# Fourier and pooling products in pieces inside the attention stage of a mixer and mixture-of-experts model

## The chip, the cores and the metric

The kernel runs on one core of one Trainium2 chip. The metric is the device time of one execution in microseconds, lower is better. All arrays are 32-bit floats, and TensorE carries out each product of the program as two instructions.

## The reference

Two blocks follow each other, and the change lies in the first. That block has two layers. A layer works on 256 tokens `x` of width 1024 and on 256 context tokens `ctx` (the second layer updates `x` alone). Cut to the part around the change:

```python
px_all = hx @ w_in[i]                       # columns: 256 Fourier, 256 pool, 512 q, 256 k, 256 v
ax = blocked_attention(qx, k_all, v_all)    # 4 query heads of 128, 2 key and value heads, 512 keys
ox = jnp.concatenate([fourier_mix(px_all[..., F_OFF:P_OFF], w_fourier[i]),
                      pool_mix(px_all[..., P_OFF:Q_OFF], w_pool[i], pool_scale[i]),
                      ax], axis=-1) @ w_out[i]
x_new = x + g1 * ox
x_new = x_new + g2 * expert_choice_ffn(modulate(x_new, norm2_g[i], sh2, sc2), ...)

def fourier_mix(f, w):      # 4 heads of 64: real part of a 2-D DFT over (tokens, head width), then @ w
    fr = jnp.real(jnp.fft.fft2(fh, axes=(-2, -1), norm="ortho"))
    return fr @ w
def pool_mix(p, w, scale):  # 4 groups of 64: mean over a window of 2, 4, 8, 16 tokens minus p, then @ w
    ...
    return y * scale
```

In the first layer the context goes through the same operations with its own 256 keys. The second block (an RWKV and mLSTM mixer with two feed-forward parts, two layers) is not touched.

## The kernel before

The program is a list of stages. Each stage is one block: every engine has its own instruction stream in it, and a barrier over all engines closes it. `block1` (line 1230 on) calls for each layer `opening_stage`, `heads_project_stage`, `attention_stage` (line 591), `fourier_pool_stage` (line 724) once for each stream of tokens (two in the first layer, one in the second), `mix_route_stage` and `moe_stage`.

Weights come through a ring of seven places of 2 MB. The order of the tiles is fixed in `build_tiles`. SyncE issues the load of a tile (line 205) when TensorE has used the tile that held its place: it waits on the semaphore `used`, which only products count up. Loads of small arrays (`dft_n`, `pool_m`, `w_fourier`, `w_pool`) are issued by ScalarE in `heads_project_stage`, before attention.

`attention_stage` goes through jobs. A job is one head and 128 query tokens: in the first layer 8 jobs over 512 keys (`kt` = 4) and then 8 over 256 keys (`kt` = 2), in the second layer 8 over 512 keys. Of job i TensorE makes the scores (line 622, issued two jobs ahead, into banks 0 and 1), VectorE takes the largest (lines 669 and 671, one job ahead), ScalarE the exponents (line 700) and, once VectorE has inverted the sum (line 678), the normalized weights (line 706). TensorE then transposes them (line 640, banks 2 and 3), ScalarE copies them out (line 716), TensorE multiplies them with the values (line 648, the output product, banks 4 and 5), and VectorE copies the output (line 662). The order on TensorE within job i is: transposes of i, scores of i + 2, output product of i. On VectorE it is: largest of i + 1, inverse of i, output copy of i - 1. Jobs 0 and 1 also carry a product of the conditioning (line 354, bank 6), which `ada_pick` (line 362) turns into columns of bank 7. The second pick and the sum that reads it (line 690) stand at the stage's end.

`fourier_pool_stage` does one stream in five steps on TensorE, each in banks of its own and each followed by a read on VectorE:

```python
 738  DFT over the head width, 4 products          -> 770 copy to G   (128 x 1024)
 744  pooling means, 8 products of 64 columns      -> 772 copy to Dp  (128 x 512)
 751  DFT over the tokens, 8 products from G       -> 774 copy to Y   (128 x 512)
 756  pooling weights, 2 products from Dp          -> 777 scaled, to mix, twice
 762  Fourier weights, 4 products from Y           -> 780 copy to mix (128 x 512)
```

`mix_route_stage` begins with the product with `w_out` (line 873), which reads all of `mix`.

Of the kernel before, what the change touches and what calls it, by code (L numbers as in the profile page):

```python
# [12 lines left out]
P = 128  # L13
# [58 lines left out]
class Core:  # L72


    def __init__(self, nc, ctx):
# [78 lines left out]
        self.rest = sig("second_half_landed")  # L154
        self.split = set()
# [435 lines left out]
def attention_stage(K, q, k, v_, jobs, prob, probT, stat, rms, mix, sil=None, rows=None, NA=0, sums=()):  # L591
# [6 lines left out]
    PRODUCT, PICKED = 6, 7  # L598

# [15 lines left out]
    with nc.Block() as block:  # L615
        @block.tensor
        def _(pe):
            def scores(i):
                h, qt, k0, kt = jobs[i]
                if i >= 2:  # L620
                    pe.wait_ge(K.dve.h, inverted(i - 2))
                K.mark(pe.matmul(K.PS[:, i % 2, 0:kt * P], q[:, h, qt * P:(qt + 1) * P],
                                 k[:, h // 2, k0:k0 + kt * P], start=True, stop=True), K.pe)

# [40 lines left out]
        def _(v):  # L665
            def largest(i):
# [7 lines left out]
            for i in range(n):  # L674
# [11 lines left out]
            if NA:  # L686
                v.wait_ge(K.pe.h, K.pe.at(n + 1))
                st = Steps(v, K.dve_order)
                for place, a, b, bias in sums:
                    st.go(v.tensor_tensor(place, columns_of(K, PICKED, a, b), bc(bias, 2, 2), ALU.add))  # L690
                st.settle()
# [29 lines left out]
    K.end()  # L721


def fourier_pool_stage(K, fp, pt, t0, W, scr, mix):


    nc = K.nc
    tile0 = t0 // P
    G = scr[:, 0:2 * 512].rearrange("p (i f) -> p i f", i=2)
    Y = scr[:, 1024:1024 + 512].rearrange("p (c t) -> p c t", c=2)  # L730
    Dp = scr[:, 1536:1536 + 512].rearrange("p (c t) -> p c t", c=2)
    with nc.Block() as block:
        @block.tensor
        def _(pe):
            K.all_loaded(pe)
            for i in range(TT):
                for c in range(2):
                    m = pe.matmul(K.PS[:, i, c * 256:(c + 1) * 256], fp[:, c, t0 + i * P:t0 + (i + 1) * P],
                                  K.dft_d, start=c == 0, stop=c == 1, skip_group_check=True)
            K.mark(m, K.pe)  # L740
            for g in range(4):
                for i in range(TT):
                    o = 64 * (g % 2)
                    m = pe.matmul(K.PS[o:o + 64, 2 + g // 2, 0:SEQ], pt[:, tile0 + i, g * 64:(g + 1) * 64],
                                  W["pool_m"][:, i, g, :], start=i == 0, stop=i == TT - 1, tile_position=(0, o))
            K.mark(m, K.pe)
            pe.wait_ge(K.dve.h, K.dve.at(1))
            for c in range(2):
                for i in range(TT):
                    for s in range(2):  # L750
                        m = pe.matmul(K.PS[:, 4 + c, 0:SEQ], G[:, i, c * 256 + s * P:c * 256 + (s + 1) * P],
                                      W["dft_n"][:, i, s, :], start=i + s == 0, stop=i + s == 2)
            K.mark(m, K.pe)
            pe.wait_ge(K.dve.h, K.dve.at(2))
            for c in range(2):
# [467 lines left out]
def block1(K, T, second_block, layers=DEPTH):  # L1223
# [9 lines left out]
    for layer in range(layers):  # L1233
# [50 lines left out]
        for s in range(streams):  # L1284
            fourier_pool_stage(K, f, pt, s * SEQ, W, scr, mix)
# [1364 lines left out]
```

## Time and profile before

| | |
|---|---|
| three runs | 3048.18, 3038.13, 3046.58 us, median 3046.58 |
| profiled execution | 3043.83 us |
| its span | 3042.0 us |
| PE busy | 2804.1 us (92%) |
| PEld busy (weight loads) | 1954.0 us (64%) |
| DVE busy | 758.0 us (25%) |
| ACT busy | 430.1 us (14%) |

The span is what the trace covers of the profiled execution; the execution's own time is 1.83 us more. PE is TensorE's products, PEld its weight loads, which run beside the products, DVE is VectorE and ACT ScalarE. The shares are means over stages of different kinds, so they don't tell what bounds the attention and Fourier stages: for that the timeline of the stretch is needed, where each row has a start, a duration and, in brackets, how long its engine had been idle before it and what ended the wait.

### The profile page before, as it was taken

The numbers are of one execution on the slowest core, as the hardware profiler recorded it, in microseconds if no ns is written. First come the engines' busy times: TensorE is split into PE (matmuls) and PEld (weight loads), VectorE is DVE, ScalarE is ACT, GpSimd is POOL, SyncE is SP. The second block draws the span as 40 slices with busy tenths as digits, with TensorE's granted clock in tenths as the row PEclk, the third lists the DMA queues.
The fourth block names the chain that finished last, engine by engine and source line by source line (L and its number), as shares of the span: only waits on it lengthen the run. The fifth ranks groups of instructions, "written<-read, shape, count | busy, mean of one in ns | idle before, by whom it ended". The sixth has DMA issues, their size and how long they took to land. (4 is left out here: it accounts for less than half of the span.)

```text
span 3042.0 us, 36506 instructions
## 1 busy us (share of the span) xinstructions
PE 2804.1 (92%) x16062; PEld 1954.0 (64%) x16062; DVE 758.0 (25%) x1522; ACT 430.1 (14%) x871; POOL 0.2 (0%) x4
## 2 busy tenths in 40 slices
PE   6989989888898988888999998999999999989998
PEld 3655434333566332223888887888888888788887
DVE  2231212111432111012111455421121143654112
ACT  2032111110222110001000312110010031211000
POOL 0000000000000000000000000000000000000000
PEclk9999999999999999999999999999999999999999
DMA  9222899999854999999335431134434453303340
GB/s 393 97 126 92 351 427 427 427 428 427 347 221 166 404 428 428 426 428 427 132 138 194 147 127 69 70 116 148 165 125 166 152 179 117 130 3 115 135 165 28
DMA packets 59383, 691.52 MB, mean 227 GB/s; under 512 B 10384, under 2 KB 13072, under 8 KB 14448
## 3 DMA queue, kind: packets, MB, share of 16 engines
q1 hardware_dynamic: 55408, 685.59, 55.9%
q10 hardware_dynamic: 3840, 3.93, 0.4%
q8 instruction: 109, 1.79, 0.2%
q14 instruction: 26, 0.21, 0.0%
HBM read 688.45 MB, written 1.05 MB: 227 GB/s over the span
## 5 line engine op out<-in xcount | busy, mean ns | idle before, releaser
L1346 PE MATMUL banks<-main,weight_ring 128*128 128x256 f32 x2560 | 559.4, 379 | 6.6 <-DVE main L1441 6.6
L1346 PEld LDWEIGHTS banks<-main,weight_ring 128*128 128x128 f32 x2560 | 486.1, 190 | 74.0 <-issue 8.1
L1052 PE MATMUL banks<-weight_ring,main 128*64 128x512 f32 (+1 forms) x1520 | 467.1, 609 | 22.4 <-DMA weight_ring<-in_up 18.1
L1357 PE MATMUL banks<-main,weight_ring 128*128 128x256 f32 x1408 | 310.4, 379 | 0.0
L1357 PEld LDWEIGHTS banks<-main,weight_ring 128*128 128x128 f32 x1408 | 267.5, 190 | 36.4
L1550 PE MATMUL banks<-main,weight_ring 128*128 128x256 f32 x1248 | 275.8, 381 | 0.0
L1078 PE MATMUL banks<-weight_ring,main 128*32 128x512 f32 (+1 forms) x752 | 239.9, 625 | 25.3 <-issue 25.3
L1550 PEld LDWEIGHTS banks<-main,weight_ring 128*128 128x128 f32 x1248 | 236.9, 191 | 36.2 <-issue 4.5
L1052 PEld LDWEIGHTS banks<-weight_ring,main 128*64 128x64 f32 (+1 forms) x1520 | 134.1, 126 | 172.9 <-issue 172.3
L1437 DVE TENSOR_TENSOR main<-banks,tmp 128x256 f32<-128x256 f32 x88 | 37.4, 425 | 697.1 <-PE banks L1346 695.2
L1168 DVE TENSOR_TENSOR main<-banks,main 64x512 f32<-64x512 f32 (+1 forms) x64 | 44.3, 692 | 504.4 <-ACT main L1140 504.4
L1419 ACT ACTIVATE main<-main 128x256 f32<-128x256 f32 x88 | 36.6, 416 | 773.6 <-DVE main L1437 773.5
L1052 PE MATMUL banks<-main 128*64 128x512 f32 (+1 forms) x256 | 119.5, 622 | 19.5 <-DMA weight_ring<-in_up 18.0
L1078 PEld LDWEIGHTS banks<-weight_ring,main 128*32 128x32 f32 (+1 forms) x752 | 70.4, 129 | 101.9 <-issue 101.9
L1052 PE MATMUL banks<-constants,main 128*32 128x512 f32 (+1 forms) x272 | 123.2, 607 | 8.1 <-DMA weight_ring<-in_up 8.1
L1173 DVE COPY main<-banks 32x512 f32<-32x512 f32 x48 | 33.1, 690 | 251.8 <-PE banks L1078 251.3
L1052 PEld LDWEIGHTS banks<-main 128*64 128x64 f32 (+1 forms) x256 | 31.4, 128 | 83.1 <-issue 80.5
L1078 PE MATMUL banks<-main 128*64 128x512 f32 (+1 forms) x160 | 73.5, 614 | 11.5 <-issue 9.9
L1052 PEld LDWEIGHTS banks<-constants,main 128*32 128x32 f32 (+1 forms) x272 | 32.6, 124 | 72.9 <-issue 72.5
L2102 PE MATMUL banks<-main 64*64 64x64 f32 x1920 | 61.6, 225 | 13.3 <-DVE main L2059 9.6
L1140 ACT ACTIVATE main<-banks 64x512 f32<-64x512 f32 (+1 forms) x64 | 37.6, 587 | 246.3 <-PE banks L1052 245.5
L2102 PEld LDWEIGHTS banks<-main 64*64 64x64 f32 x1920 | 59.9, 141 | 15.0 <-DVE main L2059 10.1
(392 smaller groups left out, 2797.1 us busy)
## 6 DMA issues: line engine op xcount, KB each, us to landing
weight_ring<-in_up SPq DMA_DIRECT2D x60, 2048.0 KB, 30.4
weight_ring<-in_down SPq DMA_DIRECT2D x45, 2048.0 KB, 28.6
weight_ring<-in_f_in SPq DMA_DIRECT2D x44, 2048.0 KB, 8.1
weight_ring<-in_gate SPq DMA_DIRECT2D x35, 2048.0 KB, 24.9
weight_ring<-in_mix_in SPq DMA_DIRECT2D x24, 2048.0 KB, 8.4
weight_ring<-in_ada_w SPq DMA_DIRECT2D x23, 2048.0 KB, 17.5
weight_ring<-in_f_out SPq DMA_DIRECT2D x44, 1024.0 KB, 4.8
constants<-in_gate SPq DMA_DIRECT2D x15, 2048.0 KB, 27.1
```

The costliest lines, as they stand in the source:

```text
L1052: m = pe.matmul(K.PS[64 * j:64 * j + S * CAP, hf, :], x, w[j][:, k, :], start=k == 0, stop=k == KC - 1, tile_position=(0, 64 * j))
L1078: m = pe.matmul(K.PS[64 * j:64 * j + S * CAP, 3 + j, :], hT[:, k, 0:S * CAP], w[j][:, k, :], start=k == 0, stop=k == KC - 1, tile_position ...
L1140: K.mark(a_.activation(hs[64:64 + S * CAP, hf, :], K.PS[0:S * CAP, hf, :], ACT.Silu), K.act)
L1168: K.mark(v.tensor_tensor(hs[64:64 + S * CAP, hf, :], K.PS[64:64 + S * CAP, hf, :], hs[64:64 + S * CAP, hf, :], ALU.mult), K.dve)
L1173: K.mark(v.tensor_copy(M.Y[e // 4 % 2][32 * (e % 4):32 * (e % 4) + 32, s, 512:1024], K.PS[64 + 32 * s:64 + 32 * s + 32, 4, :]), K.dve2)
L1346: m = pe.matmul(K.PS[:, 4 + c, g * SEQ:(g + 1) * SEQ], w[:, k, g, c * P:(c + 1) * P], H[:, k, :], start=g + k == 0, stop=g == 1 and k == K ...
L1357: m = pe.matmul(K.PS[:, o // 2, (o % 2) * SEQ:(o % 2 + 1) * SEQ], w[:, c, o * P:(o + 1) * P], hid[:, b, c, :], start=first and c == 0 and ...
L1419: a_.activation(sg[:, c, :], sg[:, c, :], ACT.Silu).then_inc(K.act.h, 1)
L1437: v.tensor_tensor(sg[:, c, :], K.PS[:, 4 + c, 0:SEQ], N.r, ALU.mult).then_inc(K.linear.h, 1)
L1550: m = pe.matmul(K.PS[:, bank(p), 0:SEQ], wt[:, k, (p % 4) * P:(p % 4 + 1) * P], H[:, k, :], start=k == 0, stop=k == KC - 1)
L2102: m = pe.matmul(K.PS[o, bank + g, (u % NH) * CH:(u % NH + 1) * CH], a[o, u, :], b[o, u, :], start=u % NH == 0, stop=c >= 2 and p == 3, ski ...
```

## The change

`fourier_pool_stage` is gone. Its work is cut into 8 pieces for each stream, and `attention_stage` issues them behind the output products of the jobs from 2 on: `pieces(i)` deals 16 pieces over 14 jobs in the first layer (one each, two behind jobs 8 and 15) and 8 pieces over 6 jobs in the second (two behind jobs 4 and 7). Pieces 0 and 1 of a stream are the DFT over the head width of one half of the tokens, 2 and 3 the means of two pooling groups, 4 and 5 the DFT over the tokens of one half of the columns, 6 the pooling weights, 7 the Fourier weights. A piece uses bank 6 or 7 in turn, and waits until the piece before last has been read. VectorE reads a piece behind the output copy of its job, before it takes the largest of the scores two jobs on. The scratch arrays move to a free part of `K.H`. The last conditioning pick moves from the stage's end to behind job 1, and its sum to VectorE's job 2. The pool scale is applied by one instruction over 2 x 256 columns instead of two.

```diff
-def attention_stage(K, q, k, v_, jobs, prob, probT, stat, rms, mix, sil=None, rows=None, NA=0, sums=()):
+def attention_stage(K, q, k, v_, jobs, prob, probT, stat, rms, mix, sil, rows, NA, sums, fp, pt, W, scr, streams):
...
+    def pieces(i):
+
+        return range((i - NA) * 8 * streams // (n - NA), (i - NA + 1) * 8 * streams // (n - NA)) if i >= NA else ()
...
+            def piece(j):
+
+                s, step, bank = j // 8, j % 8, K.PS[:, 6 + j % 2, :]
+                if j == 0:
+                    K.all_loaded(pe)
+                if j < 2:
+                    pe.wait_ge(K.turned.h, K.turned.at(1))
+                else:
+                    pe.wait_ge(K.mixread.h, K.mixread.at(j - 1))
+                if step in (0, 1):
+                    for c in range(2):
+                        m = pe.matmul(bank[:, c * 256:(c + 1) * 256], fp[:, c, s * SEQ + step * P:s * SEQ + (step + 1) * P],
+                                      K.dft_d, start=c == 0, stop=c == 1, skip_group_check=True)
...
+                else:
+                    pe.wait_ge(K.mixread.h, K.mixread.at(8 * s + 6))
...
+                K.mark(m, K.mixed)
...
-            if NA:
-                pe.wait_ge(K.even.h, K.even.at(NA))
-                K.mark(ada_pick(K, pe, rows[:, (NA - 1) % 2, :], PICKED, 8 * (NA - 1), False, True), K.pe)
+                if i == NA - 1:
+                    pe.wait_ge(K.even.h, K.even.at(NA))
+                    K.mark(ada_pick(K, pe, rows[:, (NA - 1) % 2, :], PICKED, 8 * (NA - 1), False, True), K.mean)
+                for j in pieces(i):
+                    piece(j)
...
+            def piece_read(j):
+
+                s, step, bank = j // 8, j % 8, K.PS[:, 6 + j % 2, :]
+                here = slice(s * SEQ, (s + 1) * SEQ)
+                v.wait_ge(K.mixed.h, K.mixed.at(j + 1))
...
                 if i >= 1:
                     out(v, i - 1)
+                    for j in pieces(i - 1):
+                        piece_read(j)
+                if i == NA:
+                    v.wait_ge(K.mean.h, K.mean.at(1))
+                    for place, a, b, bias in sums:
+                        K.mark(v.tensor_tensor(place, columns_of(K, PICKED, a, b), bc(bias, 2, 2), ALU.add), K.turned)
             out(v, n - 1)
+            for j in pieces(n - 1):
+                piece_read(j)
...
-def fourier_pool_stage(K, fp, pt, t0, W, scr, mix):
...
-        for s in range(streams):
-            fourier_pool_stage(K, f, pt, s * SEQ, W, scr, mix)
```

Three places show how the instructions move. The first is TensorE behind job 8 of the first layer, the first job over 256 keys. Before, its output product (648) is followed at once by job 9's transposes (640):

```order
L640 MATMUL banks<-constants,main 128x128 [waits scalar_copies_ready]
L640 MATMUL banks<-constants,main 128x128
L622 MATMUL banks<-main 128x256 [waits vector_ready]
L648 MATMUL banks<-main 128x128 [waits vector_copies_ready,scalar_copies_ready]
L648 MATMUL banks<-main 128x128
L640 MATMUL banks<-constants,main 128x128 [waits scalar_copies_ready]
```

Now (686 are the transposes, 631 the scores, 694 the output product, 661 and 667 the pooling and Fourier weights):

```order
L686 MATMUL banks<-constants,main 128x128 [waits scalar_copies_ready]
L686 MATMUL banks<-constants,main 128x128
L631 MATMUL banks<-main 128x256 [waits vector_ready]
L694 MATMUL banks<-main 128x128 [waits vector_copies_ready,scalar_copies_ready]
L694 MATMUL banks<-main 128x128
L661 MATMUL banks<-main 128x256 [waits fourier_pool_products_read]
L661 MATMUL banks<-main 128x256
L667 MATMUL banks<-main 128x256 [waits fourier_pool_products_read]
L667 MATMUL banks<-main 128x256 x3
L686 MATMUL banks<-constants,main 128x128 [waits scalar_copies_ready]
```

Two pieces with six products stand between the output product and the transposes of job 9.

The second place is VectorE between job 8 and job 10 of the first layer. Before, the output copy (662) is followed by the next largest (669):

```order
L678 RECIPROCAL small<-small 128x1 [waits scalar_ready]
L662 COPY main<-banks 128x128 [waits down_products_ready]
L669 TENSOR_REDUCE small<-banks 128x1 [waits matmuls_ready]
L671 TENSOR_SCALAR small<-small 128x1 [waits vector_ready]
L678 RECIPROCAL small<-small 128x1 [waits scalar_ready]
```

Now (743 inverts, 710 copies the output, 726 and 728 read pieces, 734 takes the largest):

```order
L743 RECIPROCAL small<-small 128x1 [waits scalar_ready]
L710 COPY main<-banks 128x128 [waits down_products_ready]
L726 TENSOR_TENSOR main<-banks,vectors 128x2x256 [waits fourier_pool_products]
L728 COPY main<-banks 128x2x256 [waits fourier_pool_products]
L734 TENSOR_REDUCE small<-banks 128x1 [waits matmuls_ready]
L736 TENSOR_SCALAR small<-small 128x1 [waits vector_ready]
```

The reads of both pieces stand ahead of the next largest, with a wait of their own each.

The third place is the end of the first layer's attention on TensorE. Before:

```order
L648 MATMUL banks<-main 128x128 [waits vector_copies_ready,scalar_copies_ready]
L648 MATMUL banks<-main 128x128
L362 MATMUL banks<-constants,main 128x2 [waits tokens_modulated]
L362 MATMUL banks<-constants,main 128x2 x3
L615 UNCONDITIONAL_BRANCH
L733 UNCONDITIONAL_BRANCH [waits barrier_Pool_Activation_PE_DVE_SP_release]
L738 MATMUL banks<-constants,main 128x256 [waits small_loads_landed]
```

Now:

```order
L694 MATMUL banks<-main 128x128 [waits vector_copies_ready,scalar_copies_ready]
L694 MATMUL banks<-main 128x128
L661 MATMUL banks<-main 128x256 [waits fourier_pool_products_read]
L661 MATMUL banks<-main 128x256
L667 MATMUL banks<-main 128x256 [waits fourier_pool_products_read]
L667 MATMUL banks<-main 128x256 x3
L624 UNCONDITIONAL_BRANCH
L859 UNCONDITIONAL_BRANCH [waits barrier_Pool_Activation_PE_DVE_SP_release]
L882 MATMUL banks<-main,constants 128x512 [waits weights_landed_6]
```

The last two pieces stand where the pick stood, and the product with `w_out` (882) follows the attention stage's barrier directly.

## Rows read from the trace of the kernel before

**Rows 1.** The page: its first line, and DMA share in 40 slices of 76 us.
```profile
span 3042.0 us, 36506 instructions
...
DMA  9222899999854999999335431134434453303340
```

**Rows 2.** Windows: busy time of each engine, then TensorE's granted clock, DMA share and GB/s.
```profile
112.00:122.00 10.00, 8.09 (x20) 3.53 (x19) 3.09 (x4) 0.00 (x0) 0.00 (x0) 1.00 0.00 0
180.00:198.00 18.00, 13.11 (x72) 8.51 (x70) 7.54 (x31) 11.72 (x33) 0.00 (x0) 1.00 0.00 1
198.00:206.00 8.00, 6.72 (x25) 5.46 (x26) 0.93 (x4) 0.38 (x1) 0.00 (x0) 0.57 0.00 0
202.10:226.87 24.77, 22.28 (x104) 16.71 (x105) 8.35 (x12) 0.00 (x0) 0.00 (x0) 0.93 0.00 1
917.09:928.67 11.58, 10.32 (x53) 7.81 (x53) 4.18 (x6) 0.00 (x0) 0.00 (x0) 1.00 0.00 0
```

**Rows 3.** Timeline, first layer, one job over 512 keys: start, duration, engine, line; idle before.
```profile
168.84 0.97 PEld L648 LDWEIGHTS banks<-main 128*128 128x128 f32 x8 [0.65 <-ACT main L716]
169.05 0.69 DVE L669 TENSOR_REDUCE small<-banks 128x1 f32<-128x512 f32 x1 [2.10 <-PE banks L622]
...
169.91 0.15 DVE L678 RECIPROCAL small<-small 128x1 f32<-128x1 f32 x1
170.10 0.72 ACT L706 ACTIVATE main<-main,small 128x512 f32<-128x512 f32 x1 [1.31 <-DVE small L678]
...
170.87 0.42 PEld L640 LDWEIGHTS banks<-constants,main 128*128 128x128 f32 x4 [1.06 <-ACT main L706]
```

**Rows 4.** Timeline, first layer, one job over 256 keys.
```profile
185.92 0.52 PEld L648 LDWEIGHTS banks<-main 128*128 128x128 f32 x4 [0.44 <-ACT main L716]
...
187.26 0.20 PEld L640 LDWEIGHTS banks<-constants,main 128*128 128x128 f32 x2 [0.82 <-ACT main L706]
...
188.17 0.42 DVE L669 TENSOR_REDUCE small<-banks 128x1 f32<-128x256 f32 x1 [1.21 <-PE banks L622]
```

**Rows 5.** Timeline, first layer: weight loads behind jobs 6, 7 and 14, and of job 15.
```profile
180.29 0.42 PEld L640 LDWEIGHTS banks<-constants,main 128*128 128x128 f32 x4 [0.37 <-ACT main L706]
...
182.76 0.20 PEld L640 LDWEIGHTS banks<-constants,main 128*128 128x128 f32 x2 [0.16 <-ACT main L706]
...
197.60 0.25 PEld L640 LDWEIGHTS banks<-constants,main 128*128 128x128 f32 x2
...
198.57 0.93 PEld L648 LDWEIGHTS banks<-main 128*128 128x128 f32 x4 [0.71 <-ACT main L716]
```

**Rows 6.** Timeline, first layer: start of the first Fourier stage, then the second.
```profile
202.10 3.60 PE L738 MATMUL banks<-constants,main 128*128 128x256 f32 x8 [0.81 <-PEq L615]
...
215.31 1.96 PE L738 MATMUL banks<-constants,main 128*128 128x256 f32 x8 [1.25 <-PEq L732]
217.20 2.00 PE L744 MATMUL banks<-main 128*64 128x256 f32 x16
...
219.13 3.72 PE L751 MATMUL banks<-main 128*128 128x256 f32 x16
...
222.89 0.69 DVE L774 COPY main<-banks 128x512 f32<-128x512 f32 x1 [2.96 <-PE banks L751]
...
223.63 1.99 PE L762 MATMUL banks<-main 128*128 128x256 f32 x8
...
225.67 0.69 DVE L780 COPY main<-banks 128x512 f32<-128x512 f32 x1 [1.04 <-PE banks L762]
...
226.87 7.11 PE L873 MATMUL banks<-main,constants 128*128 128x512 f32 x16 [1.25 <-PEq L732]
```

**Rows 7.** Timeline, second layer: weight loads of job 7's transposes and output product, then the next stage.
```profile
912.94 0.47 PEld L640 LDWEIGHTS banks<-constants,main 128*128 128x128 f32 x4
...
914.34 0.97 PEld L648 LDWEIGHTS banks<-main 128*128 128x128 f32 x8 [0.92 <-ACT main L716]
...
928.67 3.69 PE L873 MATMUL banks<-main,weight_ring 128*128 128x256 f32 x16 [1.26 <-PEq L732]
```

More of the change, by code:

```diff
@@ L154, in __init__ @@
         self.rest = sig("second_half_landed")
+        self.mixed = sig("fourier_pool_products")
+        self.mixread = sig("fourier_pool_products_read")
         self.split = set()
@@ L623, in scores @@
                                  k[:, h // 2, k0:k0 + kt * P], start=True, stop=True), K.pe)
+            def piece(j):
[10 more added lines that the diff above has]
+                                      K.dft_d, start=c == 0, stop=c == 1, skip_group_check=True)
+                elif step in (2, 3):
+                    for o in range(2):
+                        g = 2 * (step - 2) + o
+                        for t in range(TT):
+                            m = pe.matmul(bank[64 * o:64 * o + 64, 0:SEQ], pt[:, s * TT + t, g * 64:(g + 1) * 64],
+                                          W["pool_m"][:, t, g, :], start=t == 0, stop=t == TT - 1, tile_position=(0, 64 * o))
+                elif step in (4, 5):
+                    c = step - 4
+                    for t in range(TT):
+                        for part in range(2):
+                            m = pe.matmul(bank[:, 0:SEQ], G[:, t, c * 256 + part * P:c * 256 + (part + 1) * P],
+                                          W["dft_n"][:, t, part, :], start=t + part == 0, stop=t + part == 2)
+                elif step == 6:
+                    for c in range(2):
+                        m = pe.matmul(bank[:, c * 256:(c + 1) * 256], W["pool"][:, c, :], Dp[:, c, :],
+                                      start=c == 0, stop=c == 1, skip_group_check=True)
+                else:
+                    pe.wait_ge(K.mixread.h, K.mixread.at(8 * s + 6))
+                    for o in range(2):
+                        for c in range(2):
+                            m = pe.matmul(bank[:, o * 256:(o + 1) * 256], W["fourier"][:, c, o * P:(o + 1) * P], Y[:, c, :],
+                                          start=o + c == 0, stop=o + c == 2, skip_group_check=True)
+                K.mark(m, K.mixed)
             scores(0)
@@ L683, in _ @@
                     out(v, i - 1)
+                    for j in pieces(i - 1):
[4 more added lines that the diff above has]
+                        K.mark(v.tensor_tensor(place, columns_of(K, PICKED, a, b), bc(bias, 2, 2), ALU.add), K.turned)
             out(v, n - 1)
+            for j in pieces(n - 1):
+                piece_read(j)
             v.wait_ge(K.dve2.h, K.dve2.at(n))
[L686 to L691, printed above, removed]
+            v.wait_ge(K.turned.h, K.turned.at(1))
+            v.wait_ge(K.mixread.h, K.mixread.at(8 * streams))
         @block.scalar
```

70 lines of the change are left out of this document (15 added, 55 removed).

## The prediction

> **What bounds the kernel now.** I took the views in this order: page, windows, timeline.
>
> The page gives the span, 3042.0 us [rows 1]; the profiled execution took 3043.83. In that stretch of the first block which the change touches, no transfer matters: the DMA share is 0.00 from 180 us to the end of the Fourier stages [rows 2]. The weight ring is full there, and SyncE waits until TensorE has used a tile. So a microsecond saved in front of the product with `w_out` moves the next loads, and all behind them, forward by the same microsecond. The two streams of the first layer take 24.77 us in stages of their own, the one of the second 11.58 [rows 2].
>
> Within attention a loop through three engines sets the pace, and not TensorE alone. Read [rows 3] as that loop: VectorE takes the largest at 169.05 and can invert the last sum only behind it, at 169.91; ScalarE normalizes at 170.10 for 0.72; TensorE transposes at 170.87, makes the next scores, and the next largest follows. What matters is its gap. TensorE's loads end with the output product's at 168.84 + 0.97 = 169.81 and the next come at 170.87, so it idles 1.06 us, as the bracket says. In a job over 256 keys the gap is 0.82 [rows 4]. Behind job 6 it is 0.37, behind job 7 0.16, and behind job 14 none: the loads of job 15's transposes have no bracket [rows 5]. The second layer's job 6 has none either [rows 7]. The pieces are put into these gaps.
>
> **What a piece costs TensorE.** The token DFT takes 3.72 us for 16 instructions and the last step 1.99 for 8 of the same shape [rows 6]: the difference gives (3.72 - 1.99) / 8 = 0.216 for each, and 1.99 - 8 x 0.216 = 0.26 for the way out of the array. A piece of 4 such instructions (0, 1, 6) takes 0.86 us and one of 8 (4, 5, 7) 1.73. Pieces 2 and 3 are 8 narrow instructions each: (2.00 - 0.26) / 16 x 8 = 0.87 [rows 6]. Going from one kind of product to the next costs about 0.17 to 0.19: the pooling products follow at 217.20, where 215.31 + 8 x 0.216 is 217.04, and I take the larger. The transposes' own first load can run beside the piece's last product; half of its 0.20 for two [rows 4] gives back 0.10. So a short piece needs 0.95 of gap, a long one 1.82, a pair of short and long 2.68 and a pair of shorts 1.82. What doesn't fit delays the transposes, and since the loop is closed, each such delay adds up.
>
> First layer:
> - Jobs 2 to 5 (short pieces, gap 1.06): 0.
> - Job 6 (long): 1.82 - 0.37 = 1.45. Job 7 (long): 1.82 - 0.16 = 1.66.
> - Job 8 (pieces 6 and 7): 2.68 - 0.82 = 1.86.
> - Jobs 9 to 12 (short): 4 x (0.95 - 0.82) = 0.52.
> - Job 13 (long): 1.82 - 0.82 = 1.00. Job 14 (long, no gap): 1.82.
>
> That makes 8.31. VectorE adds a little. Its read of a 512-column piece takes 0.69 [rows 6] and starts 0.26 after the product. Behind jobs 2 and 3 it ends about 0.5 us before the next largest. Behind jobs 8 to 10 it comes out 0.1 to 0.2 later than the largest wants, which is due 0.91 after the transposes [rows 4]: 0.40 in all. Reads of 256 columns (0.42 by the reduction in [rows 4]) are done in time. Sum 8.71.
>
> The end: job 15's output product starts at 198.57 [rows 5], now 8.71 later. Behind it come its 4 loads 0.52 [rows 4], the change of kind 0.19, pieces 14 and 15 with 2.59, the way out 0.26, the read 0.69, and the barrier. That is 0.51, from the end of the last read, 225.67 + 0.69, to the next product, 226.87 [rows 6]. Together 4.76. The product with `w_out` starts at 198.57 + 8.71 + 4.76 = 212.04 instead of 226.87: **14.8 us saved**.
>
> Second layer: jobs 2 and 3 (short) 0, job 4 (two short pieces) 1.82 - 1.06 = 0.76, job 5 (long) 0.76, job 6 (long, no gap) 1.82: 3.34. From job 7's output product at 914.34: 0.97 + 0.19 + 2.59 + 0.26 + 0.69 + 0.51 = 5.21. So 914.34 + 3.34 + 5.21 = 922.89 instead of 928.67 [rows 7]: **5.8 us saved**.
>
> **Edits costed at nothing.** The second pick is 8 instructions with full weight loads, as the output product's 8 that take 0.97 [rows 3]. It goes behind job 1, a job over 512 keys with a gap of 1.06; without that cover it costs 0.97 a layer. Its sum waits on VectorE with the largest of job 4 behind it, which is due later than the pick ends. The wait for the small loads: the DMA engines were idle from 112 to 122 [rows 2], so they had landed long before piece 0 at about 166. One scale instruction in place of two saves VectorE a little beside other work.
>
> **Sum.** 3043.83 - 14.8 - 5.8 = 3023.2 us, rounded to 3023. The median of the three runs is 2.75 us above the profiled execution and the lowest 5.7 below it, so I keep the profiled one.
>
> **The clock.** TensorE's granted clock was 0.57 of full between 198 and 206, that is, mostly at the 1.2 GHz level, after 18 us at 2.4 in which its products kept it busy 13.1 us [rows 2]. The eight instructions at 202.10 took 3.60 there against 1.96 later [rows 6]. I have costed everything at the full level. The Trainium skill (TensorE: Matmul & The Clock Gate, What's actually happening) says that the throttled state is the default and that activity releases it; by that rule the fuller jobs hold the clock up, and my sum stands as it is. Without it the low stretch comes back, which is the first rival.
>
> **The rivals.**
> 1. *The clock falls near attention's end all the same.* For: it did, in the first layer. Against: the pieces fill most of what idle time led up to it. Price: pieces 13 to 15 and the last output product are 4.3 + 0.5 us at full clock, and at 3.60 / 1.96 = 1.84 times that they cost 4.0 more. Time 3027. The same once more in the second layer would give 3031.
> 2. *The weights take the gain back in the first layer*, because the expert stage waits for its tiles anyway. For: the DMA engines are at 9 tenths or more in the slices from the sixth to the tenth [rows 1], where the first layer's experts are. Against: those engines stand still before it, and the loads that matter start on TensorE's own signals. Price: the 14.8 us; time 3038.
> 3. *Slower: the reads close the loop.* VectorE works in order, and the next largest stands behind a read that waits for its piece. If the scores were always ready before the piece is, each piece would cost its whole chain: 0.19, product, 0.26, read. For a stream: 2 x 2.00 (pieces 0, 1) + 2 x 1.74 (2, 3) + 2 x 2.60 (4, 5) + 2.00 (6) + 2.87 (7) = 17.55, or 52.7 for three, against 24.77 + 11.58 = 36.35 removed [rows 2]. Time 3060. It decides from 1.5 us a piece on. Against: in [rows 3] a short piece's read ends at about 168.5 and the next largest starts at 169.05. The Trainium skill (TensorE: Matmul & The Clock Gate, Architectural detail) calls VectorE's queue strictly first in, first out. That is the rule that speaks against this change, and by it alone the time would be this rival's; no row of before has a wait placed like that.
>
> That the change doesn't do what it says I exclude: the order of the instructions shows the pieces in the jobs and the stages gone.
>
> **How the numbers follow.** Forecast 0.78, the first rival 0.10, the second 0.06, the third 0.03, the rest for what I don't see. The bounds of the unknown: if the changes of kind are free and the delays half of what I sum, the gain grows by 6.4 us, to 3017; a run like 3038.13 lies 5.7 lower again, so with most of both the low end is 3012. Up, the first rival in both layers gives 3031, and a median above the profiled execution a little more: 3032. A measurement of this kernel can tell about 0.3%, or 9 us, from no change. Faster by more than that holds the forecast and the first rival, 0.89 with what little the rest gives; within it is the second, 0.07; slower 0.04.
>
> **What would show it.** Right: no stage between attention and the product with `w_out`, which starts near 212 in the first layer and near 928.67 - 14.8 - 5.8 = 908 in the second. Jobs 2 to 5 keep their pace; those with a long piece grow by 0.7 to 1.8; reads wait for products and never the largest for a read by over 0.2. Granted clock 1.00 up to the stage's end. Wrong: jobs that grow by 2 us or more, VectorE's largest starting right behind a read, TensorE waiting for weights in the product with `w_out`, or a gap that opens at the expert stage.

## The result, and the profile after

The changed kernel takes 3024.64 us (median of 7 runs, the lowest 3023.0), the kernel before 3046.86 (median of 7) in the same session. The medians lie 22.2 us apart. The ratio, 0.9936, is taken without the one run of each kernel that is far off the others (14229.74 and 3342.42 us). Its 95% interval is 0.9924 to 0.9948: faster, by more than the 0.3% that the prediction counts as no change. The profiled execution took 3027.66 us, 16.2 less than the one before.

The page of the kernel after, its first line, busy times and DMA share in 40 slices (to hold beside [rows 1]):

```profile
span 3025.8 us, 36481 instructions
...
PE 2797.9 (92%) x16062; PEld 1949.8 (64%) x16062; DVE 758.1 (25%) x1528; ACT 430.3 (14%) x871; POOL 0.2 (0%) x4
...
DMA  9133899999755999998345331133434443303340
```

Windows of the kernel after. The first answers to the third of [rows 2], the others are the two layers' ends, from the last output product to the product with `w_out`:

```profile
198.00:206.00 8.00, 7.88 (x49) 5.11 (x48) 4.86 (x18) 4.78 (x14) 0.00 (x0) 1.00 0.00 0
211.03:215.69 4.66, 3.31 (x17) 2.68 (x17) 1.68 (x4) 0.00 (x0) 0.00 (x0) 1.00 0.00 0
903.01:908.11 5.10, 3.75 (x20) 3.12 (x21) 1.67 (x3) 0.00 (x0) 0.00 (x0) 1.00 0.00 0
```

The granted clock is 1.00 where it was 0.57. The DMA share is still 0.00: no transfer has become the bound.

Timeline of the kernel after, first layer, a job over 512 keys with a short piece (645 is the piece, 720 its read; for [rows 3]):

```profile
173.19 0.97 PEld L694 LDWEIGHTS banks<-main 128*128 128x128 f32 x8 [0.66 <-ACT main L785]
...
173.40 0.69 DVE L734 TENSOR_REDUCE small<-banks 128x1 f32<-128x512 f32 x1 [0.83 <-PE banks L631]
174.08 0.73 PEld L645 LDWEIGHTS banks<-constants,main 128*128 128x128 f32 x4
...
174.44 0.72 ACT L775 ACTIVATE main<-main,small 128x512 f32<-128x512 f32 x1 [1.31 <-DVE small L743]
...
175.22 0.31 PEld L686 LDWEIGHTS banks<-constants,main 128*128 128x128 f32 x3 [0.41 <-ACT main L775]
175.25 0.69 DVE L720 COPY main<-banks 128x512 f32<-128x512 f32 x1 [0.57 <-PE banks L645]
```

The piece sits in the gap. 0.41 of the 1.06 us are left, and the bracket still names ScalarE: TensorE waits for the normalization as before, and the piece is free. This job takes 3.38 us from one output product to the next, as before.

The same, job 8 with pieces 6 (661) and 7 (667), then job 9 with piece 8 (for [rows 4]):

```profile
191.06 0.52 PEld L694 LDWEIGHTS banks<-main 128*128 128x128 f32 x4 [0.44 <-ACT main L785]
191.50 0.73 PEld L661 LDWEIGHTS banks<-main 128*128 128x128 f32 x4
...
192.26 1.70 PEld L667 LDWEIGHTS banks<-main 128*128 128x128 f32 x8
...
192.48 1.89 PE L667 MATMUL banks<-main 128*128 128x256 f32 x8
...
193.99 0.36 PEld L686 LDWEIGHTS banks<-constants,main 128*128 128x128 f32 x2
...
194.41 0.69 DVE L728 COPY main<-banks 128x512 f32<-128x512 f32 x1 [1.04 <-PE banks L667]
...
195.06 0.42 DVE L734 TENSOR_REDUCE small<-banks 128x1 f32<-128x256 f32 x1
195.06 0.52 PEld L694 LDWEIGHTS banks<-main 128*128 128x128 f32 x4 [0.44 <-ACT main L785]
```

Here TensorE is full. The loads of the transposes (686) have no bracket, and the job takes 4.00 us instead of 2.24.

The end of the first layer's stage, and in the last row the second layer's next product (for [rows 5 to 7]):

```profile
211.03 0.52 PEld L694 LDWEIGHTS banks<-main 128*128 128x128 f32 x4 [0.71 <-ACT main L785]
...
212.44 1.89 PE L667 MATMUL banks<-main 128*128 128x256 f32 x8
...
214.37 0.69 DVE L728 COPY main<-banks 128x512 f32<-128x512 f32 x1 [1.03 <-PE banks L667]
...
215.69 1.52 PE L882 MATMUL banks<-main,constants 128*128 128x512 f32 x3 [1.35 <-PEq L624]
...
908.11 1.10 PE L882 MATMUL banks<-main,weight_ring 128*128 128x256 f32 x4 [1.35 <-PEq L624]
```

**Where the 16.2 us came from.** Attention began 4.35 us later in this execution (scores at 154.54 instead of 150.19), so starts can't be compared, only stretches. The last column is the time in which the trace's clock records show TensorE at the lower of its two levels (1.2 GHz, granted share 0.5), before and after:

| stretch, us | before | after | difference | of it at 1.2 GHz |
|---|---|---|---|---|
| start to first scores | 150.19 | 154.54 | +4.35 | 13.7, 23.9 |
| first layer, scores to `w_out` product | 76.68 | 61.15 | -15.53 | 10.2, 3.4 |
| from there to the second layer's scores | 656.42 | 652.80 | -3.62 | 54.6, 41.0 |
| second layer, scores to `w_out` product | 45.38 | 39.62 | -5.76 | 3.4, 3.4 |
| from there to the end | 2113.33 | 2117.69 | +4.36 | 92.3, 99.1 |

The three stretches outside attention hold the same code. In all the profiles of this document they took 149.2 to 154.5, 652.4 to 656.4 and 2109.3 to 2117.7 us. So a difference of a few us between two single spans is not a statement on the change. Most of this spread goes with the clock. At the start, the profiles with 13.7 us at the low level took 149.2 to 151.4 us, those with 17.1 took 152.4 to 153.0, and the two with 23.9 took 154.5. At the end, the six with 75.3 to 82.5 us at the low level took 2109.3 to 2110.6, the kernel before with 92.3 took 2113.3, and the five with 85.6 to 99.1 took 2115.0 to 2117.7. In the middle stretch the tie is weaker. The stretches from the first output product on, which carry the comparisons below, repeat within 0.03 us where a kernel was profiled twice.

### The profile page after: what moved, and what is told of

Its sections match the earlier page's. It is cut to its first block and busy times, and to the rows that moved or that the text cites. A ratio compares the mean times of both kernels' runs of the same rounds, so it can differ in the third digit from the quotient of the medians.

```text
span 3025.8 us, 36481 instructions
## 1 busy us (share of the span) xinstructions
PE 2797.9 (92%) x16062; PEld 1949.8 (64%) x16062; DVE 758.1 (25%) x1528; ACT 430.3 (14%) x871; POOL 0.2 (0%) x4
## 5 line engine op out<-in xcount | busy, mean ns | idle before, releaser
L1061 PE MATMUL banks<-main 128*64 128x512 f32 (+1 forms) x256 | 116.2, 608 | 18.1 <-DMA weight_ring<-in_up 16.5
L1087 PE MATMUL banks<-main 128*64 128x512 f32 (+1 forms) x160 | 70.4, 592 | 12.8 <-issue 11.1
## 6 DMA issues: line engine op xcount, KB each, us to landing
weight_ring<-in_down SPq DMA_DIRECT2D x45, 2048.0 KB, 28.1
```

The costliest lines, as they stand in the source:

```text
L1061: m = pe.matmul(K.PS[64 * j:64 * j + S * CAP, hf, :], x, w[j][:, k, :], start=k == 0, stop=k == KC - 1, tile_position=(0, 64 * j))
L1087: m = pe.matmul(K.PS[64 * j:64 * j + S * CAP, 3 + j, :], hT[:, k, 0:S * CAP], w[j][:, k, :], start=k == 0, stop=k == KC - 1, tile_position ...
```

## The experiments

"L0" and "L1" are the stretches from the first output product of attention to the product with `w_out`, in the first and second layer, of each kernel's profile. The fifth column adds their differences from before. The last two columns compare the times with those of the kernel before in the same session; its median was 3046.86 beside the first row, 3043.64 beside "last pieces ahead, again" and "all pieces ahead", 3045.15 beside "reads ahead", "gaps filled", "wide pooling" and "each piece twice", and 3044.66 beside the rest. Each stretch is read from one profiled execution.

| kernel | median us | L0 | L1 | L0 + L1 less before | ratio | 95% |
|---|---|---|---|---|---|---|
| before | | 69.94 | 38.65 | | | |
| after | 3024.64 | 54.42 | 32.78 | -21.4 | 0.9936 | 0.9924 to 0.9948 |
| after, once more | 3022.89 | 54.39 | 32.76 | -21.4 | 0.9932 | 0.9918 to 0.9945 |
| first layer only | 3024.60 | 54.41 | 37.90 | -16.3 | 0.9940 | 0.9927 to 0.9952 |
| second layer only | 3036.18 | 69.17 | 32.77 | -6.7 | 0.9970 | 0.9959 to 0.9981 |
| reads ahead of the inverse | 3049.77 | 73.33 | 42.17 | +6.9 | 1.0019 | 1.0008 to 1.0030 |
| before, gaps filled | 3041.51 | 67.21 | 40.28 | -1.1 | 0.9995 | 0.9983 to 1.0006 |
| last pieces ahead | 3016.96 | 52.56 | 30.36 | -25.7 | 0.9911 | 0.9896 to 0.9925 |
| last pieces ahead, again | 3016.52 | 52.57 | 30.37 | -25.7 | 0.9915 | 0.9901 to 0.9929 |
| wide pooling | 3021.82 (one run) | 53.63 | 32.42 | -22.5 | | |
| each piece twice | 3049.15 | 73.11 | 41.81 | +6.3 | 1.0014 | 1.0004 to 1.0025 |
| all pieces ahead | 3014.57 | 50.26 | 30.23 | -28.1 | 0.9906 | 0.9892 to 0.9919 |

The differences of the stretches and those of the times agree within the intervals (1% is 30 us), so the stretches can be used for what a median can't tell apart.

### One layer alone

The kernel after, with `fourier_pool_stage` of before put back for one layer:

```diff
-                        ..., K.H[:, 1024:3072], streams)
+                        ..., K.H[:, 1024:3072], streams if layer == 0 else 0)
+        if not (layer == 0):
+            for s in range(streams):
+                fourier_pool_stage(K, f, pt, s * SEQ, W, K.H[:, 1024:3072], mix)
```

> Pieces inside attention in the first layer alone; the second layer keeps a Fourier stage of its own. My theory (each layer's gain is local and arrives in full at the end): from the first output product of the first layer's attention to the product with w_out 54.4 us as in the changed kernel, against 69.9 before, and 38.7 in the second layer as before; time 15.5 us below before, about 3031. If the weights take the gain back in the expert stage, the first layer's stretch is 54.4 all the same but the time is within 3 us of before.

The other kernel has `layer == 1` in both places. (In both, a layer without pieces makes none in attention: `pieces(i)` is empty there.)

> Pieces inside attention in the second layer alone. My theory: the second layer's stretch from the first output product to the product with w_out is 32.8 us against 38.7 before, the first layer's 69.9 as before; time 5.9 us below before, about 3040. If the first layer's gain were lost to the weights, this run would be as fast as the changed kernel, 3025.

First layer only: L0 54.41, L1 37.90. Second only: L0 69.17, L1 32.77. The layers add up: 15.53 + 5.88 is the whole change's 21.4. By the times alone they would not: the two kernels are 20.1 and 8.5 us below before (medians) where 15.5 and 5.9 were expected, but the intervals, 14.6 to 22.2 and 5.8 to 12.5 us, hold both expectations. The layer without pieces is 0.75 or 0.77 shorter than before too. What still differs there is the second pick, which moved from the stage's end to behind job 1, and the place of the scratch arrays. The jobs of that layer take what they took before and all of the difference is at its end, where the pick stood. So of the gain 1.5 us are the pick's, and the rest go with the pieces, the clock's share (next experiment) among them. Nothing behind the first layer took its gain back (rival 2): w_out to the second layer's scores is 652.84 with pieces in the first layer.

In the kernel with pieces in the second layer only, the low clock is back where it was before (window, to hold beside the same one of after):

```profile
198.00:206.00 8.00, 6.67 (x25) 4.39 (x26) 1.65 (x3) 0.38 (x1) 0.00 (x0) 0.57 0.00 0
```

### The clock, without the change

The kernel before, with two unread products (four instructions, a short piece's cost) behind each of the first layer's jobs 8 to 13:

```diff
                 K.mark(m, K.pe2)
+                if n == 16 and 8 <= i < 14:
+                    pe.wait_ge(K.even.h, K.even.at(NA))
+                    for c in range(2):
+                        pe.matmul(K.PS[:, PRODUCT, c * 256:(c + 1) * 256], k[:, 0, 0:P], q[:, 0, 0:256], ...)
```

> The kernel before, with two products behind the output products of jobs 8 to 13 of the first layer that nobody reads; nothing else is changed. My theory on the clock: with these gaps filled the granted clock stays at 1.00 between 198 and 206 us (0.57 before), the first Fourier stage takes 11.6 us as the second does instead of 13.2, and the stretch from the last output product to it shrinks by 1.2; 2.8 us less in the stretch, at a cost of 0.1 for the products. If the low clock there has nothing to do with the gaps, it is low again and the stretch is 0.1 to 1 longer.

Windows of this kernel (the first two answer to [rows 2]):

```profile
180.00:198.00 18.00, 16.87 (x94) 12.26 (x94) 7.54 (x31) 11.70 (x33) 0.00 (x0) 1.00 0.00 1
198.00:206.00 8.00, 6.72 (x43) 5.24 (x43) 2.58 (x5) 0.39 (x1) 0.00 (x0) 1.00 0.00 0
912.00:918.00 6.00, 6.00 (x28) 4.03 (x28) 1.92 (x2) 0.00 (x0) 0.00 (x0) 0.72 0.00 0
```

24 more instructions on TensorE cost the jobs 0.02 us each (2.27 instead of 2.25), the clock stayed at 1.00, and L0 fell by 2.73 us where 2.7 was expected. In the second layer, which the edit doesn't touch, a low clock appeared at 912 to 918, where the kernel before has none, and L1 grew by 1.63. The time is the same as before's (0.9983 to 1.0006). So filling the gaps held the clock here, in the one profiled execution, and about 2.7 of the 15.5 us that the first layer gained are what the low stretch had cost; but a low stretch can come up elsewhere.

### Where the read waits

The kernel after, with the reads of the pieces ahead of the inverse of the next sum:

```diff
                     largest(i + 1)
+                for j in pieces(i - 1):
+                    piece_read(j)
                 v.wait_ge(K.act.h, K.act.at(i + 1))
                 K.mark(v.reciprocal(stat[:, i, 3:4], stat[:, i, 2:3]), K.dve)
...
                     out(v, i - 1)
-                    for j in pieces(i - 1):
-                        piece_read(j)
```

> The changed kernel, with VectorE's reads of a piece moved ahead of the inverse of the next sum instead of behind the output copy. Nothing else moves, and TensorE's order stays. My theory (it is the place of the waiting read in VectorE's queue that keeps it harmless): the inverse now waits for the piece and its read, so each of the 12 middle jobs of the first layer and 5 of the second grow by about 1.6 us; together 27 us, time about 3051, slower than before. If a read that waits costs nothing wherever it stands, because the loop has slack, the time stays at 3025.

3049.77 us, 1.0019 of before (1.0008 to 1.0030): slightly slower than before, as expected. The same kind of job as above, from its timeline (745 is the inverse):

```profile
168.69 1.03 PE L645 MATMUL banks<-constants,main 128*128 128x256 f32 x4
169.76 0.69 DVE L720 COPY main<-banks 128x512 f32<-128x512 f32 x1 [0.91 <-PE banks L645]
170.37 0.15 DVE L745 RECIPROCAL small<-small 128x1 f32<-128x1 f32 x1
...
170.55 0.72 ACT L775 ACTIVATE main<-main,small 128x512 f32<-128x512 f32 x1 [2.91 <-DVE small L745]
...
171.32 0.42 PEld L686 LDWEIGHTS banks<-constants,main 128*128 128x128 f32 x4 [2.01 <-ACT main L775]
```

The inverse waits behind the read, and the normalization and the transposes with it: 2.01 us of idle time on TensorE instead of 0.41. Jobs 2 to 5 take 4.97, 4.98, 4.88 and 4.87 us instead of 3.37 to 3.46. The same 24 instructions of VectorE, moved ahead of the inverse and the output copy, cost 73.33 - 54.42 = 18.9 us in the first layer and 42.17 - 32.78 = 9.4 in the second, 28.3 together where 27 was expected. Not all of it is the queue's: the second layer has a low clock near its end (0.84 from 924 to 930 us), which after has not, and that end is 1.66 us longer; 26.6 are left. That is the third rival's mechanism, and it is real, at less than that rival's price (6.9 us above before by the stretches, not 16). The change avoids it by where its reads stand.

### Doubling the pieces

The kernel after, with the products of every piece issued twice with the same values:

```diff
+                for again in range(2):
-                if step in (0, 1):
+                    if step in (0, 1):
...
                 K.mark(m, K.mixed)
```

> The changed kernel, with the products of every piece issued twice into the same bank (the second time overwrites the first with the same values). My theory (the gaps are used up and each delay in the loop adds up): of the 28.5 us of added products all but about 1 us appears: 27.5 more than the changed kernel, 3052, slower than before. If the pieces still had free gaps around them, half of it at most.

L0 grew by 18.7 us, L1 by 9.0: 27.7 where 27.5 was expected. By the forecast's prices a stream's second set is 3 x 0.86 + 2 x 0.87 + 3 x 1.73 = 9.51, so 19.0 and 9.5: nearly all of it is on the path, since one set has used most of the cover. Only behind jobs 2 and 3 a second short piece costs less than its 0.86 (4.01 us instead of 3.37). The loop does not close, even with pieces of 3.6 us. Timeline, from job 8 (668 is piece 7, 631 the scores, 729 the read, 735 the largest):

```profile
198.13 3.43 PEld L668 LDWEIGHTS banks<-main 128*128 128x128 f32 x16
...
201.58 0.36 PEld L687 LDWEIGHTS banks<-constants,main 128*128 128x128 f32 x2
...
202.00 0.69 DVE L729 COPY main<-banks 128x512 f32<-128x512 f32 x1 [2.76 <-PE banks L668]
202.01 0.60 PE L631 MATMUL banks<-main 128*128 128x256 f32 x2
...
202.65 0.42 DVE L735 TENSOR_REDUCE small<-banks 128x1 f32<-128x256 f32 x1
```

The largest that stands behind the read needs scores that TensorE makes behind the piece and the transposes. They are done at 202.01 + 0.60 = 202.61, the read is over at 202.69, and the largest starts at 202.65. That is 0.04 us after the scores, about as long as where the read is done early (scores at 212.37, largest at 212.40 in this kernel). However long the piece is, read and scores both start from its end, so the read holds the largest up by next to nothing.

### The narrow pieces

The kernel after, with pieces 2 and 3 as two products over all 128 columns instead of four over 64:

```diff
-                    for o in range(2):
-                        g = 2 * (step - 2) + o
-                        for t in range(TT):
-                            m = pe.matmul(bank[64 * o:64 * o + 64, 0:SEQ], pt[..., g * 64:(g + 1) * 64], ..., tile_position=(0, 64 * o))
+                    g = 2 * (step - 2)
+                    for t in range(TT):
+                        m = pe.matmul(bank[:, 0:SEQ], pt[:, s * TT + t, g * 64:(g + 2) * 64], W["pool_m"][:, t, g, :], ...)
```

> The changed kernel, with pieces 2 and 3 as two products over all 128 columns of the stationary operand instead of four over 64 (both groups of a piece then get the first group's window, which changes what the pooling computes). My theory on jobs 4, 5, 11 and 12 (the loads of the transposes start beside a running product of full width but only after narrow ones have ended): jobs 11 and 12 fall from 2.58 us to 2.27 as jobs 9 and 10, jobs 4 and 5 from 3.46 to 3.38, job 4 of the second layer from 4.37 to 4.0. If it is the length of the piece, nothing changes, for both forms take 0.86.

This form gives both groups of a piece the window of the first, so it serves to time the form and not as a kernel. L0 fell by 0.79, L1 by 0.36. Jobs 11 and 12 take 2.27 us, jobs 4 and 5 take 3.38, and job 4 of the second layer 4.01, all as expected. The job behind which piece 10 stands, in the kernel after (651 the piece, narrow):

```profile
200.24 0.64 PEld L651 LDWEIGHTS banks<-main 128*64 128x64 f32 x8
200.25 1.09 PE L651 MATMUL banks<-main 128*64 128x256 f32 x8
...
200.38 0.51 ACT L775 ACTIVATE main<-main,small 128x256 f32<-128x256 f32 x1 [0.83 <-DVE small L743]
...
201.27 0.20 PEld L686 LDWEIGHTS banks<-constants,main 128*128 128x128 f32 x2 [0.39 <-ACT main L775]
```

and in the kernel with the wide form (650 the piece, 774 the normalization, 685 the transposes):

```profile
196.81 1.03 PE L650 MATMUL banks<-main 128*128 128x256 f32 x4
...
197.04 0.51 ACT L774 ACTIVATE main<-main,small 128x256 f32<-128x256 f32 x1 [0.83 <-DVE small L742]
...
197.60 0.22 PEld L685 LDWEIGHTS banks<-constants,main 128*128 128x128 f32 x2 [0.16 <-ACT main L774]
```

The bracket names ScalarE both times. With the wide piece the loads start 0.05 us behind the end of the normalization (197.55); with the narrow piece 0.38 behind it (200.89), just before the narrow products end (201.34). So the full-width loads were not waiting for ScalarE but for the narrow products. The length of the piece and its number of instructions are not it. Behind piece 7, also 8 instructions but of full width, the loads start at 193.99, which is 0.38 us before its products end (192.48 + 1.89). And with each piece twice, behind 16 narrow products (652), the loads of the transposes (687) wait again until just before these end, though the normalization was over at 210.20:

```profile
209.56 2.00 PE L652 MATMUL banks<-main 128*64 128x256 f32 x16
...
211.49 0.20 PEld L687 LDWEIGHTS banks<-constants,main 128*128 128x128 f32 x2 [0.39 <-issue]
```

In all 15 such places of the kernels after, after once more and each piece twice the loads start 0.07 us before the last narrow product's end as the trace models it. That costs 2.57 - 2.27 = 0.30 us in a 256-key job, 0.08 in a 512-key job whose gap is longer, and 4.37 - 4.01 = 0.36 in the second layer's job with two of them.

### The stage's end

The kernel after, with the last two jobs' pieces ahead of their output product, and their reads ahead of the output copy:

```diff
+                if i >= n - 2:
+                    for j in pieces(i):
+                        piece(j)
                 pe.wait_ge(K.act2.h, K.act2.at(2 * i + 2))
...
-            out(v, n - 1)
             for j in pieces(n - 1):
                 piece_read(j)
+            out(v, n - 1)
```

> The changed kernel, with the pieces of the last two jobs of a layer ahead of their output products instead of behind them, where TensorE waits for ScalarE's copy, and read ahead of the output copies. My theory (TensorE has no gap in these jobs, so whatever fills its wait for the copy is gained, and the stage then ends with a copy of 128 columns instead of 512): 1.6 us less in the first layer, 2.0 in the second, 3.6 in all, 3021. If VectorE's reads or the end barrier set the stage's end, it gains nothing.

Timeline of this kernel, the first layer's end (661 and 667 pieces, 697 the output product, 732 the last read):

```profile
205.17 1.89 PE L667 MATMUL banks<-main 128*128 128x256 f32 x8
...
206.69 0.63 PEld L697 LDWEIGHTS banks<-main 128*128 128x128 f32 x4
...
207.10 0.69 DVE L732 COPY main<-banks 128x512 f32<-128x512 f32 x1 [1.04 <-PE banks L667]
207.71 0.28 DVE L714 COPY main<-banks 128x128 f32<-128x128 f32 x1
...
208.52 3.67 PE L890 MATMUL banks<-main,constants 128*128 128x512 f32 x8 [1.01 <-PEq L624]
```

TensorE waited 0.71 us for ScalarE's copy ahead of the last output product (row 211.03 of after); the pieces now fill that wait, and the output product covers the read of the last piece. L0 fell by 1.86 and L1 by 2.42 us (expected 1.6 and 2.0), and the ratio, 0.9911, lies below both of the changed kernel's (0.9936 and 0.9932). The intervals still overlap, by at most 0.0011 with the second measurement, 0.9915, so it is the stretches that show the gain and the times that agree with it.

The same for every job:

```diff
+                for j in pieces(i):
+                    piece(j)
                 pe.wait_ge(K.act2.h, K.act2.at(2 * i + 2))
...
-                    out(v, i - 1)
                     for j in pieces(i - 1):
                         piece_read(j)
+                    out(v, i - 1)
```

> As e5_tail, but in all jobs the pieces stand ahead of the output product, between the scores and the wait for ScalarE's copy, and are read ahead of the output copy. My theory (the output product is off the loop, and behind 256-column scores TensorE waits some 0.3 to 0.4 us for that copy, which a piece can fill; behind 512-column scores it hardly waits): jobs 6, 7, 8, 11, 12 and 13 of the first layer each lose about 0.3, nothing changes in the second layer; 2 us less than e5_tail, stretch of the first layer 50.6. If the output product is needed sooner than I think, because VectorE copies it ahead of the next largest, the jobs grow instead.

> e5_tail again, on the same chip as e8_all_ahead. Both theories: stretches of 52.6 us in the first layer and 30.4 in the second, time about 4 us below the changed kernel, 3019.

> The changed kernel again, beside the others on one chip. Both theories: 0.9936 of before within its interval, 3025 us; jobs 2 and 3 of the first layer at 3.37 us, job 8 at 4.0, jobs 11 and 12 at 2.58.

3014.57 us, the fastest of all, 0.9906 of before, against 3016.52 for the last pieces alone on the same chip. L0 is 2.31 us shorter again, L1 only 0.14. Timeline, first layer, a job over 512 keys (696 the output product):

```profile
171.06 1.03 PE L645 MATMUL banks<-constants,main 128*128 128x256 f32 x4
...
171.71 1.07 PEld L696 LDWEIGHTS banks<-main 128*128 128x128 f32 x8
...
172.19 0.67 DVE L720 COPY main<-banks 128x512 f32<-128x512 f32 x1
```

A job has two gaps on TensorE: about 1.06 us ahead of the transposes and 0.65 ahead of the output product (0.82 and 0.44 over 256 keys). A piece ahead of the output product delays that product and uses the second gap, and what is left over still falls into the first. The first piece makes the step from one output product to the next 4.24 us instead of 3.38, but that costs nothing: from transposes to transposes the same job takes 3.37 us as before. Counted from transposes to transposes, jobs 6, 7, 8, 11, 12 and 13 lose 0.39, 0.52, 0.31, 0.33, 0.26 and 0.15 us against the last pieces alone, where about 0.3 each was expected. So it is worth most with long pieces and with the narrow ones, behind which the output product now waits and not the transposes. The interval of this kernel overlaps that of the last pieces alone; by the times the two are not told apart, only by the stretches.

## Why the prediction was right

The forecast was 3023 us with a range of 3012 to 3032; measured were 3024.64 and, again, 3022.89. The forecast gain was 20.6 us. The stretches show 21.4. The terms (in L0 and L1 each delay is the growth of the step from one output product to the next):

| term | forecast | measured |
|---|---|---|
| L0, jobs 2 and 3 | 0 | 0 |
| L0, jobs 4 and 5 (narrow) | 0 | 0.08 each |
| L0, jobs 6, 7, 8 | 1.45, 1.66, 1.86 | 1.33, 1.54, 1.76 |
| L0, jobs 9 and 10 | 0.13 each | 0.02 each |
| L0, jobs 11 and 12 (narrow) | 0.13 each | 0.33 each |
| L0, jobs 13 and 14 | 1.00, 1.82 | 0.89, 1.73 |
| L0, reads on VectorE | 0.40 | 0 |
| L0, sum of the delays | 8.71 | 8.11 |
| L0, end | 4.76 | 4.66 |
| L1, jobs 4, 5, 6 | 0.76, 0.76, 1.82 | 1.00, 0.63, 1.73 |
| L1, end | 5.21 | 5.10 |
| saved in L0 / L1 | 14.8 / 5.8 | 15.5 / 5.9 |

- **The loop and its gaps** held. Jobs 2 and 3 kept their pace, and the long pieces cost what stood out of the gap.
- **The price of a piece** was right to 0.1 us. The 0.17 to 0.19 for a change of kind was too high for wide products: each long piece came out about 0.1 cheaper. In the other direction the narrow pieces' way out was missing: I had taken 0.87 for them and no more. Both errors nearly cancelled, and that is luck: in the first layer the wide pieces came out 0.76 us cheaper in all, the narrow ones 0.56 dearer. At the stage's end the same happened on a smaller scale: the barrier took 0.63 us in the changed kernel (214.37 + 0.69 to 215.69) and not 0.51, and the rest of the end 0.22 less than summed.
- **VectorE's 0.40** was a term that isn't there. The read behind job 9 starts at 196.68 and lasts 0.69, and the next largest starts at 197.33; its scores are done at 197.29. I had set the read's end against a largest that would have come on time without the piece; but the scores are delayed by the same piece. For the same reason one of the signs of being wrong was badly chosen: the largest does start right behind a read (195.06, behind 194.41 + 0.69), and it means nothing here, since its scores were not done before 195.02.
- **Edits costed at nothing**: the wait for the small loads was free. The second pick behind job 1 was too (that job takes 3.38 us in both kernels), and that it left the end is inside the forecast of the two ends; it measured 0.75 and 0.77.
- **The clock** (rival 1) stayed at 1.00 up to the stage's end wherever pieces were dealt out, in every kernel but the one with the reads ahead, and there it failed in the second layer only. The Trainium skill (TensorE: Matmul & The Clock Gate, What's actually happening) has activity release the throttle, and the filled kernel of before agrees: 1.00 instead of 0.57. But the kernel with the reads ahead does not fit such an account. In the first layer its TensorE was busy 6.11 of the 10 us from 200 to 210, against 13.11 of 18 before the low stretch of before [rows 2], and its clock stayed up (the window from 198 to 206):

```profile
198.00:206.00 8.00, 5.66 (x28) 4.15 (x28) 3.69 (x11) 1.49 (x5) 0.00 (x0) 1.00 0.00 0
```

  So that the pieces hold the clock because they fill the gaps is likely for these two kernels and no rule. What brings a low stretch on stays open.
- **Rival 2** (the weights take it back) fell: L0's gain is in the time of the kernel with the first layer alone, 0.9940.
- **Rival 3** (the reads close the loop) was set up with a condition that this order can't meet. I had it decide from 1.5 us a piece on; at twice the products and 3.6 us it still didn't. With another order it comes at once. The Trainium skill (TensorE: Matmul & The Clock Gate, Architectural detail) has VectorE's queue strictly first in, first out. The run with the reads ahead agrees, with some 27 us; but the rule alone doesn't say what the read holds up. That depends on whether the instruction behind it needs something that comes later than the piece anyway.
- The forecast for the whole, 14.8 + 5.8 = 20.6 us, was not what the profiled execution showed (16.2). Its attention stretches show 21.3, and the medians 22.2. The missing 5 us are in stretches that the change doesn't touch, and there they go mostly with the clock: 10.2 us more at the low level ahead of attention and 6.8 more behind the second layer's product with `w_out`. That this product starts at 908.11, as forecast to 0.1 us, is luck: attention began 4.35 us later, and the stretch between the layers took 3.62 less. In the second profile of the same kernel it starts at 904.13.

## What to carry to other kernels

- Price extra work by the gap of the engine it goes to, job by job, not by the busy share: here a piece with 0.86 us of products was free in a gap of 1.06 and cost 0.02 in one of 0.82, and the second copy of all the pieces cost 27.7 of its 28.5 us.
- A read that must wait belongs ahead of an instruction whose own input comes later than that read's, and never ahead of one whose input is ready sooner, where that one is in the loop that sets the pace. The same reads two instructions earlier turned 22 us of gain into 5 of loss.
- At a stage's end put the filler ahead of the last dependent product, so that the product covers the filler's read: 1.9 and 2.4 us here, for a change of order alone.

## What the runs showed of the hardware that I had not expected

- Full-width weight loads start only as products of 64 columns end: in one 256-key job 0.38 us after their data were ready, against 0.05 with the wide form of the same piece. Behind full-width products they start 0.38 us before these end. The trace's bracket names the engine that had delivered the data, and so hides it; the wide form of the same piece shows it.
- A low-clock stretch of TensorE moves from place to place between kernels. Filling the gaps of the first layer removed one at 198 to 206 us (2.7 us), and one appeared at 912 to 918, some 700 us away from the edit (1.6 us). All the profiles have another in the experts' part, 10.3 us long, which begins 41 to 43 us behind the second layer's product with `w_out` (in the changed kernel from 950.4 to 960.6). Five of them, the changed kernel's two among them, have a further one soon after it, which the kernel before and the one with the first layer alone have not:

```profile
964.00:974.00 10.00, 10.00 (x40) 3.20 (x42) 0.59 (x1) 1.67 (x2) 0.00 (x0) 0.83 0.41 159
```

- The same five are the ones that take longest from that product to the end, the same code in all: 2115.0 to 2117.7 us, against 2109.3 to 2113.3 for the others. The whole spread is 8.4 us, more than the second layer's gain. It follows the time at the low level (75 to 99 us), though what brings a low stretch on isn't shown. That is why the stretches and not the spans carry this document.
